# The second block's mixers, reordered: attention units beside the dense tiles, the inverse for two chunk pairs in turn, the state chain beside a two-pass output product, one scale for two norms

## The chip, the cores and the metric
One core of one Trainium2 chip runs the whole program. The metric is the device time of one execution in microseconds (us). Names in the rows: PE is TensorE's matmuls, PEld its weight loads, DVE is VectorE, ACT ScalarE, POOL GpSimd, SP SyncE (it issues the weight loads from memory).

## The reference
Two transformer blocks on 256 tokens (272 with 16 meta tokens in the first) of 1024 features, all in fp32. The change touches only the second block and the norms between the two:

```python
x = first_block(...)                       # ends in rms_norm(h, final_norm)
u = rms_norm(h, norm1_g)                   # the next norm follows at once
p_rwkv, p_nsa = split(u @ w_in)            # 1024 -> 3072 (+ gates)
y = concat([rwkv7_time_mix(p_rwkv), nsa_attention(p_nsa)])
h = h + y @ w_out
h = h + swiglu(rms_norm(h, norm2_g), w_gate, w_up, w_down)
return rms_norm(h, norm_f_g)
```

`rwkv7_time_mix`: 8 heads of 64; per token t the state is `S = S * w_t + (S @ a_t) b_t + v_t k_t`, the output `y_t = S r_t`, then a norm by head, a bonus term and a gate. `nsa_attention`: 8 query and 2 key/value heads; a compressed branch (14 or 15 blocks of 32 tokens), a selected branch and a window branch. With 256 tokens and 4 selection blocks the last two both attend causally to everything; each has a gate per token and head.

## The kernel before
**Layout.** Features lie on the 128 partitions, tokens along the free axis. Every dense product is taken in three fp32r products (`part_products`, L588 to L590: high weight x high activation, high x low, low x high). ScalarE rounds a weight tile of 128x1024 to its high part (`split_hi`, L1247), VectorE subtracts to get the low part (`split_lo`, L1637); four slots hold split tiles, so the splits run four tiles ahead of TensorE. SP fills a ring of two 1 MB blocks (two tiles each), a block being issued when both tiles of the block two before it are split. The small products of the mixers are plain fp32.

**Order.** Five instruction streams are written out by hand and meet by semaphores; each engine runs its stream in order. Around the change they are:

- *Norms.* After the first feed-forward, VectorE adds the down product to `res` (L1875); ScalarE squares each tile twice, plain (L1429) and times the gain norm3 (L1430); TensorE sums both over the partitions (L866, L867). ScalarE takes root and inverse of the first, VectorE multiplies them into the second sum (L1886), ScalarE takes its root, VectorE joins the two scales (L1889). Then VectorE scales tile by tile (L1892), ScalarE rounds, VectorE takes the rest (L1645), and TensorE starts tile 0 of the second projection. VectorE then writes the normed `res` (eight products, L1898) before the first token shift.
- *Second projection, 25 tiles.* Their order is lora and gate inputs, RWKV keys, r and values, then the attention's. TensorE's stream lays RWKV work between tiles: lora products (L900 to L908), head sums (`sums_by_head`, L922), turned tokens and, at tiles 13 to 15, the masked products of each chunk of 64 tokens (L932, L935), then from tile 16 the inverse of a triangular 64x64 matrix per head and chunk in five levels: `join_products(level)`, a copy by ScalarE, `inverse_terms(level)`, an addition by VectorE (L1933, L1936), each for all 4 chunks at once. These are `by_head` products (L886): 32 calls of 64x64 for all chunks, heads two at a time. `hidden` (L970) is the compressed branch's first layer, beside tiles 21 to 24. GpSimd does part of the elementwise work (masks, identity, decays, carried states).
- *After the projection.* Eight attention units (2 branches x 4 query heads per group): scores (L1059, L1063), VectorE's fused bias and maximum (`nsa_maxima`, L2015), ScalarE's exps (L1561), VectorE's scaling of the rows (`nsa_scaled`, L2031), six transposes (L1075), ScalarE's copy (L1596), values (`nsa_values`, L1093), and VectorE's copy out (`nsa_kept`, L2039, L2041). Between the units lie the state's steps, chunk by chunk: `carry_sa`, `sa_grows`, `carry_state`, `state_grows`, and the output of a pair of chunks (`outputs`, L1120 to L1127, `output_sums`, L1133) with its norm, and the compressed branch (L1139 to L1164).
- *Output product.* Eight tiles of the full depth of 8 input tiles, the attended ones first (`MIXER_ORDER`), then the squares of the second norm (L855) and the feed-forward (L603, L605), unchanged by the change.

The lines that carry the inverse before:

```python
by_head(2, lambda c, j: nl[:, c * PAIRS + j, :], lambda c, j, hs: xi[hs, c * PAIRS + j, :])   # join_products
dve.tensor_tensor(xi.rearrange(flat3), both(4), xi.rearrange(flat3), ALU.add)                 # grow
```

## Time and profile before
| | us |
|---|---|
| three runs | 869.26, 864.61, 856.50 |
| median | 864.61 |
| profiled execution | 856.46 |
| its span, first to last instruction | 854.3 |

The span and the 2.2 us around it make the execution's time. The page gives busy time per engine, slices of 21.4 us in tenths, the chain of work that ended last, and groups of instructions by line. A busy TensorE is not one at its peak: the granted clock is 1.0 at 2.4 GHz and 0.5 at 1.2 GHz, and a value between is a mixture over the stretch.

### The profile page before, as it was taken

Reading aid. Unit: us, or ns where it says so; the run is one execution under the profiler, and the core shown is the slowest. Engines: PE = TensorE matmul, PEld = TensorE weight load, DVE = VectorE, ACT = ScalarE, POOL = GpSimd, SP = SyncE. Lnnn points to the kernel's source line nnn. Section 1 sums busy time; section 2 is a strip of 40 time slices with the busy share of each in tenths; the row PEclk is TensorE's granted clock in tenths of the full one; section 3 lists DMA queues with packets and bytes.
Section 4 is the critical chain, followed back from the end, with each engine's and each line's share of the span. In section 5 each row is a group of like instructions: output and inputs, shape, how many; then the busy total and the mean of one; then the engine's idle time right before and its main releaser. Section 6 shows DMA issues by size and latency. Waiting matters only on the chain.

```text
span 854.3 us, 16426 instructions
## 1 busy us (share of the span) xinstructions
PE 783.9 (92%) x6614; PEld 691.8 (81%) x6614; DVE 516.4 (60%) x907; ACT 410.4 (48%) x707; POOL 48.8 (6%) x44
## 2 busy tenths in 40 slices
PE   5999799799999999997989999966589999999996
PEld 4997555398888889996879898854479888889996
DVE  4556433256989995446679442444445999997443
ACT  5334224446656664336763262433445766666332
POOL 0000000000000000000116340010000000000000
PEclk9999778799999999998999999967679999999999
DMA  5644200024765555542333124200114555555541
GB/s 208 248 160 149 86 0 1 0 100 140 259 233 186 208 184 190 196 171 75 100 114 133 52 101 153 99 1 1 50 51 148 197 198 196 179 181 185 193 147 49
DMA packets 16738, 113.65 MB, mean 133 GB/s; under 512 B 2000, under 2 KB 2128, under 8 KB 3632
## 3 DMA queue, kind: packets, MB, share of 16 engines
q1 hardware_dynamic: 15984, 109.22, 36.4%
q0 software_dynamic: 704, 3.71, 1.3%
q8 instruction: 38, 0.62, 0.3%
q14 instruction: 12, 0.10, 0.0%
HBM read 111.87 MB, written 1.05 MB: 132 GB/s over the span
## 4 chain that ended last, share of the span: by engine, by line
PE 82%; DVE 10%; ACT 4%; issue 2%; POOL 1%; DMA 1%; SPq 0%; DVEq 0%; ACTq 0%; POOLq 0%
PE ps L603 19%; PE ps L588 11%; PE ps L590 10%; PE ps L589 10%; PE ps L605 10%; PE ps L886 5%; DVE w_lo L1637 2%; PE ps L1075 1%; ACT w_hi L1247 1%; PE ps L1093 1%; PE ps L743 1%; PE ps L741 1%; PE ps L768 1%; PE ps L855 1%; DVE arena L2015 1%
## 5 line engine op out<-in xcount | busy, mean ns | idle before, releaser
L1637 DVE TENSOR_TENSOR w_lo<-ring,w_hi 128x1024 fp32r<-128x1024 f32 x194 | 248.1, 1279 | 138.2 <-ACT w_hi L1247 136.8
L1247 ACT ACTIVATE w_hi<-ring 128x1024 fp32r<-128x1024 f32 x194 | 204.7, 1057 | 148.2 <-PE ps L590 132.1
L603 PE MATMUL ps<-acts,w_hi 128*128 128x512 f32 x704 | 246.7, 394 | 0.0
L605 PE MATMUL ps<-acts,w_lo 128*128 128x256 f32 x704 | 197.4, 280 | 0.0
L588 PE MATMUL ps<-acts,w_hi 128*128 128x256 f32 (+1 forms) x496 | 149.3, 301 | 18.5 <-DVE acts L1645 13.5
L603 PEld LDWEIGHTS ps<-acts,w_hi 128*128 128x128 f32 x704 | 132.1, 188 | 30.0
L589 PE MATMUL ps<-acts,w_hi 128*128 128x256 f32 (+1 forms) x496 | 144.6, 292 | 0.0
L590 PE MATMUL ps<-acts,w_lo 128*128 128x256 f32 (+1 forms) x496 | 144.6, 291 | 0.0
L605 PEld LDWEIGHTS ps<-acts,w_lo 128*128 128x128 f32 x704 | 132.3, 188 | 0.1
L588 PEld LDWEIGHTS ps<-acts,w_hi 128*128 128x128 f32 x496 | 97.5, 197 | 25.5 <-issue 18.1
L588 PE MATMUL ps<-hid_hi,w_hi 128*128 (+1 forms) x352 | 99.6, 283 | 0.0
L589 PE MATMUL ps<-hid_lo,w_hi 128*128 (+1 forms) x352 | 99.6, 283 | 0.0
L590 PE MATMUL ps<-hid_hi,w_lo 128*128 (+1 forms) x352 | 99.6, 283 | 0.0
L589 PEld LDWEIGHTS ps<-acts,w_hi 128*128 128x128 f32 x496 | 97.8, 197 | 0.5 <-issue 0.5
L590 PEld LDWEIGHTS ps<-acts,w_lo 128*128 128x128 f32 x496 | 97.8, 197 | 0.0
L588 PEld LDWEIGHTS ps<-hid_hi,w_hi 128*128 128x128 f32 x352 | 67.6, 192 | 0.1
L590 PEld LDWEIGHTS ps<-hid_hi,w_lo 128*128 128x128 f32 x352 | 67.6, 192 | 0.0
L589 PEld LDWEIGHTS ps<-hid_lo,w_hi 128*128 128x128 f32 x352 | 67.6, 192 | 0.0
L1403 ACT ACTIVATE hid_hi<-f 128x256 f32 (+1 forms) x44 | 18.4, 419 | 30.3 <-DVE f L1846 30.3
L1396 ACT ACTIVATE yT<-ps 128x256 f32<-128x256 f32 x44 | 16.6, 377 | 23.4 <-PE ps L605 23.4
L1391 ACT ACTIVATE yT<-ps 128x256 f32<-128x256 f32 x44 | 16.6, 378 | 19.0 <-PE ps L605 18.7
L1828 DVE TENSOR_TENSOR yT<-ps,yT 128x256 f32<-128x256 f32 x44 | 18.5, 422 | 8.3 <-ACT yT L1391 8.3
(338 smaller groups left out, 947.0 us busy)
## 6 DMA issues: line engine op xcount, KB each, us to landing
ring<-in_weights SPq DMA_DIRECT2D x101, 1024.0 KB, 4.8
res<-in_xT SPq DMA_DIRECT2D x2, 544.0 KB, 4.3
ring<-in_weights SPq DMA_DIRECT2D x2, 512.0 KB, 4.5
cst<-in_consts POOLq DMA_DIRECT2D x1, 1024.0 KB, 5.4
out_features<-yT SPq DMA_DIRECT2D x4, 256.0 KB, 2.1
cst<-in_consts POOLq DMA_DIRECT2D x1, 817.5 KB, 4.5
vec<-in_vecs POOLq DMA_DIRECT2D x1, 677.5 KB, 4.3
cst<-in_consts POOLq DMA_DIRECT2D x1, 656.0 KB, 5.6
```

The source lines that it names most:

```text
L588: pe.matmul(dst, w_hi[:, slot, k, :], hi, start=first, stop=False, skip_group_check=True)
L589: pe.matmul(dst, w_hi[:, slot, k, :], lo, start=False, stop=False, skip_group_check=True)
L590: return pe.matmul(dst, w_lo[:, slot, k, :], hi, start=False, stop=last, skip_group_check=True)
L603: pe.matmul(ps[:, bank, :].rearrange("p (x t) -> p x t", x=2), w_hi[:, slot, k, :], acts[:, :, k, 0:SEQ], start=(k == 0), stop=(k == KT - ...
L605: return pe.matmul(ps[:, bank, 0:SEQ], w_lo[:, slot, k, :], act_hi[:, k, 0:SEQ], start=False, stop=(k == KT - 1), skip_group_check=True)
L886: mm = pe.matmul(ps[hs, bank + n // 8, (n % 8) * HD:(n % 8 + 1) * HD], lhs(c, j)[hs], rhs(c, j, hs), start=True, stop=True)
L1247: act.activation(w_hi[:, t % SLOTS].rearrange("p k c -> p (k c)"), ring[:, b % RING, half].rearrange("p k c -> p (k c)"), ACT.Copy)\
L1391: act.activation(cross[:, m, 0, :], ps[:, 2 * m, SEQ:2 * SEQ], ACT.Copy).then_inc(S("gate_crossed"), 1)
L1396: act.activation(cross[:, m, 1, :], ps[:, 2 * m + 1, SEQ:2 * SEQ], ACT.Copy).then_inc(S("up_crossed"), 1)
L1403: act.activation(dst, sig2[:, m, :], ACT.Copy).then_inc(S("hid_rounded"), 1)
L1637: dve.tensor_tensor(w_lo[:, t % SLOTS].rearrange("p k c -> p (k c)"), ring[:, b % RING, half].rearrange("p k c -> p (k c)"), w_hi[:, t % S ...
L1828: dve.tensor_tensor(gated[:, m, :], ps[:, 2 * m, 0:SEQ], cross[:, m, 0, :], ALU.add)\
```

## The change
- **Norms.** ScalarE scales the squares with a gain that folds both epsilons (`gain_eps`, made by two small activations behind two small VectorE products), one set of sums gives the one scale that the projection needs. The plain squares go to a buffer of their own; five are made ahead of the root and three between the roundings, their sums are taken by TensorE behind the first and within tile 0. `split_hi` of tile 3 now stands behind the root in ScalarE's stream; VectorE's `split_lo` of it stays ahead of its wait for the root. The eight products that write the normed `res` go under tiles 5, 7, 9 and 11.
- **Projection.** The attention's tiles come right after the gates, RWKV's behind them, the compressed branch's last. The eight units run beside tiles 7 to 25: scores before odd tiles, the turn before even ones, values two odd tiles later. The rows are no longer scaled: the probabilities are the stationary operand, the output comes by token, and VectorE scales its 64-column pieces as it adds them up (`nsa_kept`, before even tiles).
- **RWKV behind the projection.** GpSimd's part goes to VectorE and ScalarE (GpSimd keeps its memsets). The chunk products, then the five levels for two pairs of chunks in turn. VectorE's mask and addition become one masked copy out of PSUM (`copy_predicated`, `fill`) into a matrix that starts as identity. ScalarE copies each token set of a pair in 512 columns (`keep_tokens`, in the order of TensorE's list) and each join (`keep_join`), with one `gather_blocks` ahead of tile 24's copy and one behind it. `hidden` and the compressed branch lie between levels; ScalarE's three activations of its hidden layer stand behind the copy of `key_values(0)`.
- **State chain.** The kept state is added by TensorE (identity product) in place of GpSimd; the decay is applied as VectorE copies out (`keep_state`). The attended sums are transposed back (`nsa_features`).
- **Output product in two passes.** The attended half of the depth goes first, into four banks, beside the state chain; the RWKV half follows. The weight blocks are laid out to match; the second norm's squares and roundings follow in pairs of tiles, six of its eight sums ahead of the first gate product.

```diff
-WA0, G0, GL0, K0, R0, V0, KC0, VC0, VS1, VW1, Q0, KS1, KW1 = 0, 1, 2, 3, 7, 11, 15, 16, 17, 18, 19, 23, 24
-MIXED = 15
+WA0, G0, GL0, KS1, VS1, Q0, KW1, VW1, K0, R0, V0, KC0, VC0 = 0, 1, 2, 3, 4, 5, 9, 10, 11, 15, 19, 23, 24
+MIXED = 14
+OUT2_BANKS = (3, 6, 7, 2)
 TILES2 = 25
@@ TensorE: tiles of the second projection
+            def plain_sum(k):
+                pe.wait_ge(S("plain_squares"), k + 1)
+                mm = pe.matmul(ps[:, 2, 0:SEQ], C("ones"), sq_plain[:, k, :], start=(k == 0), stop=(k == KT - 1),
+                               skip_group_check=True)
+                if k == KT - 1:
+                    mm.then_inc(S("plain_sums"), 1)
+            for k in range(5):
+                plain_sum(k)
...
+            def nsa_values(u):
+                br = u // GQA
+                pe.wait_ge(S("nsa_weights"), u + 1)
+                pe.wait_ge(S("values_kept"), br + 1)
+                if u > 0:
+                    pe.wait_ge(S("nsa_out_kept"), u)
+                for t in range(2):
+                    for g in range(KVH):
+                        dst = ps[:, 7, (t * KVH + g) * HD:(t * KVH + g + 1) * HD]
+                        for kt in range(t + 1):
+                            w0 = (t + kt) * P
+                            mm = pe.matmul(dst, pt_nsa[:, g, w0:w0 + P], vt_nsa[:, br, kt, grp(g)],
+                                           start=(kt == 0), stop=(kt == t), skip_group_check=True)
...
+            pe.wait_ge(S("late_tables_landed"), 48)
+            for t in range(TILES2):
+                if t == 3:
+                    decay_and_rate()
+                if t == 4:
+                    gates()
+                if t == 6:
+                    pe.wait_ge(S("lora_sigmoids"), 1)
+                    turn_values(VS1, True)
+                if t == 12:
+                    turn_values(VW1, False)
+                if t == 14:
+                    pe.wait_ge(S("values_kept"), 2)
+                    pe.wait_ge(S("key_squares"), 2)
+                    sums_by_head(scr, 0, "key_sums")
+                if t == 16:
+                    pe.wait_ge(S("key_sums_kept"), 1)
+                    pe.wait_ge(S("key_squares"), 4)
+                    sums_by_head(scr, 1, "key_sums")
+                if t % 2 and 0 <= (t - 7) // 2 < UNITS:
+                    nsa_scores((t - 7) // 2)
+                if t % 2 == 0 and 0 <= (t - 10) // 2 < UNITS:
+                    nsa_turn((t - 10) // 2)
+                if t % 2 and 0 <= (t - 11) // 2 < UNITS:
+                    nsa_values((t - 11) // 2)
+                pe.wait_ge(S("w_split"), T_IN2 + t + 1)
...
+                        if 2 <= k < 5:
+                            plain_sum(k + 3)
@@ TensorE: the inverse, two chunk pairs in turn
+            def joined(m, level):
+                if level == 1:
+                    pe.wait_ge(S("products_masked"), 2 * m + 2)
+                    if m == 0:
+                        pe.wait_ge(S("tokens_kept"), 1)
+                else:
+                    pe.wait_ge(S(f"xi_grown_{m}"), level - 1)
+                by_head((3, 6)[m], lambda c, j: wtb[:, c * PAIRS + j, 0:HD], lambda c, j, hs: xi[hs, c * PAIRS + j, :],
+                        PAIR[m]).then_inc(S(f"joins_{m}"), 1)
...
+            joined(0, 1)
+            bonus(0)
+            grow_xi(0, 1)
+            joined(1, 1)
+            grow_xt(0, 1)
+            bonus(1)
+            grow_xi(1, 1)
+            joined(0, 2)
+            grow_xt(1, 1)
+            hidden(2)
+            hidden(3)
+            grow_xi(0, 2)
+            joined(1, 2)
+            grow_xt(0, 2)
+            pe.wait_ge(S("bonus_kept"), 2)
+            value_tokens(0)
+            grow_xi(1, 2)
+            joined(0, 3)
+            grow_xt(1, 2)
+            value_tokens(1)
+            cmp_folded()
+            grow_xi(0, 3)
+            joined(1, 3)
+            grow_xt(0, 3)
+            key_values(0)
+            cmp_compressed()
+            grow_xi(1, 3)
+            joined(0, 4)
+            grow_xt(1, 3)
+            key_values(1)
+            grow_xi(0, 4)
+            joined(1, 4)
+            grow_xt(0, 4)
+            turn_tokens(2, ar[:, 0], 1)
+            grow_xi(1, 4)
+            joined(0, 5)
+            pe.wait_ge(S("xi_grown_0"), 4)
+            cmp_scores(0)
+            grow_xt(1, 4)
+            turn_tokens(2, bb, 0)
+            joined(1, 5)
+            grow_xt(0, 5)
+            turn_tokens(2, bb, 1)
+            turn_tokens(2, key_raw, 0)
@@ TensorE: state chain, output product
+            def state_ahead(c):
+                if c > 0:
+                    pe.wait_ge(S("state_grown"), c)
+                    by_head(1, lambda c, j: C("eye64"), lambda c, j, hs: states[hs, c - 1, j, :], (c,), (c % 2) * SEQ,
+                            start=True, stop=False)
+                by_head(1, lambda c, j: k_tok[:, c * PAIRS + j, :], lambda c, j, hs: v_tok[hs, c * PAIRS + j, :], (c,),
+                        (c % 2) * SEQ, start=(c == 0), stop=False)
+            def state_after(c):
+                pe.wait_ge(S("sa_kept"), c + 1)
+                by_head(1, lambda c, j: b_tok[:, c * PAIRS + j, :], lambda c, j, hs: sa[hs, c * PAIRS + j, :], (c,),
+                        (c % 2) * SEQ, start=False).then_inc(S("state_terms"), 1)
...
+            def out_part(half, n, x):
+                t = T_OUT2 + 4 * half + n
+                if x == 0:
+                    pe.wait_ge(S("w_split"), t + 1)
+                for kq in range(4):
+                    k = (4, 0)[half] + kq
+                    mm = part_products(ps[:, OUT2_BANKS[n], x * SEQ:(x + 1) * SEQ], t % SLOTS, 4 * x + kq,
+                                       act_hi[:, k, 0:SEQ], act_lo[:, k, 0:SEQ],
+                                       half == 0 and x == 0 and kq == 0, half == 1 and kq == 3)
+                    if half == 1 and n == 3 and x == 1 and kq < 3:
+                        mm.then_inc(S("act_used"), 1)
...
+            pe.wait_ge(S("tokens_kept"), 8)
+            pe.wait_ge(S("xt_grown_0"), LEVELS - 1)
+            pe.wait_ge(S("cmp_vector"), 3)
+            own_sa(0)
+            own_sa(1).then_inc(S("sa_terms"), 1)
+            from_state(1, 2, 3)
+            turn_tokens(2, key_raw, 1)
+            cmp_turn()
+            pe.wait_ge(S("tokens_kept"), 9)
+            state_ahead(0)
+            pe.wait_ge(S("xt_grown_1"), LEVELS - 1)
+            own_sa(2)
+            own_sa(3)
+            from_state(2, 4, 6)
+            state_after(0)
+            pe.wait_ge(S("tokens_kept"), 10)
+            cmp_values(2)
+            pe.wait_ge(S("w1_kept"), 1)
+            sa_of(1)
+            state_ahead(1)
+            state_after(1)
+            nsa_features(2)
+            pe.wait_ge(S("w1_kept"), 2)
+            sa_of(2)
+            state_ahead(2)
+            outputs(0)
+            state_after(2)
+            pe.wait_ge(S("normed"), normed("mixer2", 3))
+            out_part(0, 0, 0)
+            sa_of(3)
+            out_part(0, 0, 1)
+            output_sums(0, 0)
+            out_part(0, 1, 0)
+            pe.wait_ge(S("sa_kept"), 4)
+            pe.wait_ge(S("y_weighted"), 1)
+            outputs(1)
+            out_part(0, 1, 1)
+            out_part(0, 2, 0)
+            output_sums(1, 4)
+            out_part(0, 2, 1)
+            out_part(0, 3, 0)
+            out_part(0, 3, 1)
+            pe.wait_ge(S("normed"), normed("mixer2", KT - 1))
+            for n in range(4):
+                out_part(1, n, 0)
+                out_part(1, n, 1)
@@ ScalarE: norms
+            act.wait_ge(S("gains_squared"), 1)
+            step(act.activation(gain_eps[:], gain_eps[:], ACT.Ln, bias=C("eps")))
+            step(act.activation(gain_eps[:], gain_eps[:], ACT.Exp, scale=0.5))
             for k in range(KT):
                 act.wait_ge(S("down_added"), k + 1)
-                act.activation(sq[:, k, 0:SEQ], res[:, k, META:CTX], ACT.Square)
-                act.activation(sq_gained[:, k, :], res[:, k, META:CTX], ACT.Square, scale=V("norm3", k))\
+                act.activation(sq_gained[:, k, :], res[:, k, META:CTX], ACT.Square, scale=gain_eps[:, k:k + 1])\
...
+            def plain_square(k):
+                act.activation(sq_plain[:, k, :], res[:, k, META:CTX], ACT.Square).then_inc(S("plain_squares"), 1)
+            for k in range(5):
+                plain_square(k)
+            act.wait_ge(S("norm_sums"), nth("norm3"))
+            step(act.activation(nrm[:, 0, 0:SEQ], ps[:, 3, 0:SEQ], ACT.Ln, bias=C("eps_twice"), scale=1.0 / D))
+            act.activation(nrm[:, 0, 0:SEQ], nrm[:, 0, 0:SEQ], ACT.Exp, scale=-0.5).then_inc(S("norm_root"), 1)
             split_hi(T_IN2 + SLOTS - 1)
-            act.wait_ge(S("norm_squares"), nth("norm3") * KT)
-            act.wait_ge(S("norm_sums"), nth("norm3"))
@@ VectorE: norms
+            dve.tensor_tensor(gain34[:], V("norm3", 0, KT), V("norm4", 0, KT), ALU.mult)
+            dve.tensor_tensor(gain_eps[:], V("norm3", 0, KT), V("norm3", 0, KT), ALU.mult)\
+                .then_inc(S("gains_squared"), 1)
             add_down(1)
             split_lo(T_IN2 + SLOTS - 1)
-            step(dve.tensor_tensor(gain34[:], V("norm3", 0, KT), V("norm4", 0, KT), ALU.mult))
             dve.wait_ge(S("norm_root"), nth("norm3"))
-            signal(dve, dve.tensor_tensor(nrm[:, 0, 0:SEQ], ps[:, 3, SEQ:2 * SEQ], nrm[:, 0, 0:SEQ], ALU.mult),
-                   "norm4_mean")
-            dve.wait_ge(S("norm4_root"), 1)
-            step(dve.tensor_tensor(nrm[:, 0, 0:SEQ], nrm[:, 0, 0:SEQ], nrm[:, 1, 0:SEQ], ALU.mult))
@@ VectorE: units kept, masked fills, end of the mixers
-                else:
-                    dve.wait_ge(S("tokens_kept"), 6)
-                dve.tensor_tensor(states[:, c - 1], ps[:, 3, SEQ:2 * SEQ].rearrange("p (j v) -> p j v", j=PAIRS),
-                                  kvd[:, n, :], ALU.add).then_inc(S("state_grown"), 1)
-            def sa_grows(c):
+                for t in range(2):
+                    for g in range(KVH):
+                        src = ps[:, 7, (t * KVH + g) * HD:(t * KVH + g + 1) * HD]
...
+            def fill(x, mask, m, level, bank):
+                n = slice(2 * m * PAIRS, 2 * (m + 1) * PAIRS)
+                mask = C(mask)[:, level * HD:(level + 1) * HD].bitcast(I32).unsqueeze(1)
+                return dve.copy_predicated(x[:, n, :], mask.to_broadcast([P, 2 * PAIRS, HD]),
+                                           ps[:, bank, :].rearrange("p (n v) -> p n v", n=2 * PAIRS))
...
+            keep_sa(0)
+            keep_state(0)
+            split_lo(T_OUT2 + 1)
+            keep_sa(1)
+            dve.wait_ge(S("cmp_products"), 5)
+            for t in range(2):
+                ins = dve.tensor_tensor(nsa_acc[:, t, :], ps[:, (7, 2)[t], :], nsa_acc[:, t, :], ALU.add)
+            ins.then_inc(S("cmp_vector"), 1)
+            keep_state(1)
+            split_lo(T_OUT2 + 2)
+            keep_sa(2)
+            for a in range(2):
+                rest_attended(a)
+            keep_state(2)
+            for a in range(2, GQA):
+                rest_attended(a)
+            keep_sa(3)
+            y_weighted(0)
             split_lo(T_OUT2 + 3)
-            y_scaled(1)
-            for at in range(1, 4):
-                rest("mixer2", MIXER_ORDER[2][at], SEQ, yT, at)
-            mixer_output(2, T_OUT2)
+            y_finished(0)
+            y_weighted(1)
+            split_lo(T_OUT2 + 4)
+            rest_out(0)
+            y_finished(1)
+            split_lo(T_OUT2 + 5)
+            rest_out(1)
+            split_lo(T_OUT2 + 6)
+            split_lo(T_OUT2 + 7)
+            output_to_gates2()
```

## Rows read from the trace of the kernel before

**Rows 1.** The page: busy time of the engines, then TensorE and its clock in slices.
```profile
PE 783.9 (92%) x6614; PEld 691.8 (81%) x6614; DVE 516.4 (60%) x907; ACT 410.4 (48%) x707; POOL 48.8 (6%) x44
...
PE   5999799799999999997989999966589999999996
...
PEclk9999778799999999998999999967679999999999
```

**Rows 2.** Busy time by stretch: start:end, length, busy of each engine, clock, DMA.
```profile
397.90:403.40 5.50, 5.45 (x25) 5.39 (x26) 5.35 (x15) 3.58 (x7) 0.58 (x1) 0.54 0.00 0
403.40:480.00 76.60, 69.65 (x842) 65.63 (x841) 56.05 (x68) 40.49 (x63) 28.03 (x23) 0.98 0.30 99
444.00:462.00 18.00, 17.26 (x312) 16.42 (x311) 17.91 (x17) 7.24 (x9) 10.71 (x4) 1.00 0.34 119
480.00:542.00 62.00, 62.00 (x1248) 56.97 (x1247) 19.59 (x18) 21.73 (x35) 10.19 (x5) 1.00 0.37 129
557.00:630.50 73.50, 45.68 (x480) 35.20 (x480) 33.98 (x126) 27.14 (x73) 5.00 (x5) 0.70 0.06 20
```

**Rows 3.** Timeline of TensorE: start, length, line; idle before and its releaser.
```profile
397.95 0.55 PE L588 MATMUL ps<-acts,w_hi 128*128 128x256 f32 x1 [5.06 <-DVE acts L1645]
```

**Rows 4.** Chain that ended last, 455 to 545: start, length, engine, line, instructions.
```profile
458.25 0.44 PE ps L932 x8
458.68 0.11 PE ps L935 x4
...
486.65 1.91 PE ps L922 x4
...
507.24 0.31 PE ps L588
...
510.27 5.75 PE ps L886 x192
...
516.02 1.00 PE ps L970 x16
...
541.96 2.01 PE ps L886 x64
```

**Rows 5.** The same chain, 550 to 590.
```profile
550.53 0.42 PE ps L1059 x4
550.95 0.43 PE ps L1063 x4
...
555.45 0.88 PE ps L1075 x6
...
556.94 1.89 PE ps L1156 x32
...
585.95 0.83 PE ps L1093 x12
```

**Rows 6.** Timelines of ScalarE and VectorE, the split of weight tile 3.
```profile
390.50 1.04 ACT L1247 ACTIVATE w_hi<-ring 128x1024 fp32r<-128x1024 f32 x1
...
391.58 1.23 DVE L1637 TENSOR_TENSOR w_lo<-ring,w_hi 128x1024 fp32r<-128x1024 f32 x1 [4.45 <-ACT w_hi L1247]
```

**Rows 7.** VectorE by line and shape, 402 to 660: count | busy, mean ns.
```profile
L1637 DVE TENSOR_TENSOR w_lo<-ring,w_hi 128x1024 fp32r<-128x1024 f32 x32 | 50.0, 1562 | 32.6 <-ACT w_hi L1247 32.5
...
L1933 DVE TENSOR_TENSOR f<-ps,f 128x1024 f32<-128x1024 f32 x4 | 4.9, 1218 | 12.7 <-PE ps L886 12.7
...
L1915 DVE TENSOR_TENSOR arena<-ps,cst 128x512 f32<-128x512 f32 x4 | 2.7, 685 | 0.0
...
L1951 DVE TENSOR_TENSOR_SCAN scratch<-arena,f 128x1024 f32<-128x1024 f32 x1 | 2.3, 2289 | 0.0
```

**Rows 8.** ScalarE's exps (L1561) alone: stretch, length, busy (instructions), clock.
```profile
542.00:630.50 88.50, 14.90 (x64) 0.75 0.07 22
```

**Rows 9.** The chain, 653 to 658.
```profile
654.32 3.02 PE ps L855 x14
```

**Rows 10.** The page: issues of weight blocks, KB each, us to landing.
```profile
ring<-in_weights SPq DMA_DIRECT2D x101, 1024.0 KB, 4.8
```

1260 lines of the change are left out of this document (618 added, 642 removed).

## The prediction

> **What bounds the kernel now.** I read the page first: TensorE is busy 783.9 of 854.3 us and no other engine over 60% [rows 1], so the end moves only if TensorE gets less work, idles less, or runs at its higher clock more. The slices say where it falls short: a few early ones, in a part that the change leaves alone, one near the middle, and four in a row from about 555 to 640 us, with TensorE at 5 to 8 tenths and the clock at 6 or 7 [rows 1]. The table by stretch makes that numbers [rows 2]. From 557.0 to 630.5 TensorE is busy 45.7 of 73.5 us at a mean clock of 0.70; from 480 to 542 it is busy all 62.0 at 1.00. From 403.4 to 480, tiles and mixer work in turn, it idles 6.9 us (76.6 less 69.7). Ahead of tile 0 of the second projection it idles 5.06 us on the norms [rows 3]. In the bad stretch each attention unit is a ring PE, DVE, ACT, PE (scores, maxima, exps, scaling, turn, weights, values) with a wait at each hand-over, and little else lies between.
>
> **Is the work itself less?** Hardly. I price TensorE's blocks at full clock. A dense tile is 3.03 us beside fp32 work (507.24 to 510.27), a "set" of head products (32 fp32 calls, 64 instructions) 2.01 us alone and 1.92 in a run (5.75 for three), a `hidden` 1.0, products of a chunk 2.2 (four times 0.44 and the 0.11 behind it), `sums_by_head` twice 1.91 [rows 4]. An attention unit: scores 0.42+0.43, six transposes 0.88, values 0.83 [rows 5].
> The inverse keeps its 14 sets. The other head products are 9.25 sets before and 10 after (the kept state goes in by an identity product). New are 8 transposes of the attended tokens, 8 x 0.147 = 1.2 us. Compressed values are 8 products of 128 columns before, 2 of 512 after: equal columns. `cmp_folded` halves, under 1 us less. So the work is 1 to 2 us more; the gain must come from lost time.
>
> **Norms before tile 0.** Before: sums of 16 calls at 0.43 from 385.7 end at 392.9, then come Ln, Exp, Exp, product, Ln, Exp, product, scale and round, and the first matmul at 397.95 [rows 3]; DVE scaled the first tile 1.6 before, at 396.35. After: one set of 8 sums. ACT squares each in 0.40 (16 squares alternate from 384.85 to 390.5 when the split starts [rows 6]; those with a gain are the slower), so from 385.2 they end at 388.5; two tiny gain steps are added in front (0.3 us, in the 385.2). Then five plain squares (0.31 each) stand in ACT's queue ahead of Ln: 390.1; Ln and Exp: 391.0. But `split_hi` of tile 3 now stands behind that Exp and DVE has `split_lo` of the same tile ahead of its wait for the root, so both, once hidden under the sums, are on the path: 1.04 and 1.2 us [rows 6], 393.3. First matmul 1.6 later, 394.9: 3.0 us earlier, where 5.3 was to be had. Inside tile 0 three plain sums are added; a clock of 0.54 there [rows 2] makes them 0.86 each, of which the DVE pace of 0.73 per step covers little: +1.6. Tile 0 ends at 402.0, 1.4 us earlier. Bounds: 0 (all eaten) and 3.
>
> **Tile 0's end to tile 24's end**, 403.4 to 541.9 before [rows 2, 4], 138.5 us. Its blocks sum to 129.6 (24 tiles 72.7, 19 sets 36.5, products 8.8, the rest 11.6), so 8.9 were lost, which checks the prices. After: 72.7 + lora and gates 3.5 + turns of values 0.9 + key sums 1.9 + eight scores 6.8 + eight turns 7.0 + seven values 5.8 = 98.6. Do the units fit under two tiles (8.5 us)? ACT: 2 x (0.4+1.05) copies and splits, exps 1.9 (14.9 for eight [rows 8]), weights 0.8 (768 columns at the split's pace), extras 0.5 = 6.1. DVE: splits 2.4, shifts 0.9, maxima 1.7, keeping 1.2, extras 1 to 4: mostly under 8.5, at tiles 17 to 21 just over, which the lead of four split tiles absorbs. The tight link is ACT: behind an odd tile it needs 0.4+1.05+1.9+0.8 = 4.15 us to deliver the weights, and TensorE comes for them after 0.88+3.03+0.85 = 4.76. I add 1 us. The eight norm3 products (3.2 us behind tile 0's rounding), which held up the first shift and with it the tanh, move under tiles 5 to 11; that wait of TensorE, under 1 us, is among the 8.9 lost before and goes. GpSimd's work leaves; in the old mixers splits of 1.2 us [rows 6] took 1.56 in the mean [rows 7]. DVE gains slack by that, no time of its own. Tile 24 ends at 402.0+98.6+1 = 501.6. The cover is thin: without it this stage gives back 13 us (rival 2).
>
> **Tile 24 to the end of the output product**, 541.9 to 654.3 before [rows 4, 9]. After: products 8.8, last values 0.8, 24 sets at 1.94 46.5, `hidden` 4.0, bonus 1.9, compressed branch 5.8, transposes 1.2, outputs 88 calls x 0.063 = 5.5, their sums 1.7, output product 192 x 0.119 = 22.8 [rows 4, 5]: 99.0. In the order of the queues I find these waits: copy of tile 24 behind `gather_blocks` (0.7; five copies of a block's strided columns, 2.7 us); `cmp_compressed` behind ACT's key-value copy and three small activations (2.0); a token copy late (0.6); the first output half behind DVE's last two rests, which are queued behind a state (1.3); `nsa_features` (0.4). Sum 5. Four more hand-overs per step of two chains, not seen by me, get 3. The masked fills (`copy_predicated`, 512 columns from PSUM) stand in no row: below 0.6 (half of the 1024 add at 1.22), above 1.15 (half the scan at 2.29) [rows 7]. I take 0.7, the masked product of 512 columns (0.69), the nearest row. Even 1.15 hides: four fills per level, 4.6 us, under some 8 us of TensorE work, each wanted two blocks later; it shows once, at 0.5. The twelve rounds of level work alternate between the pairs, so each copy (0.6) lies beside a block of 1.0 of the other pair. End: 501.6+99.0+5+3 = 608.6.
> The weights stay ahead: a 1 MB block lands 4.8 us after its issue [rows 10]. SP issues output block 2 when DVE has split the second output tile, about 565, and it is needed from 594 on; the first gate block goes out when output tile 5 is split, about 594, for 612. `hidden` blocks 2 and 3 are issued when the first two are used, about 510, for 522. A load late by its whole 4.8 us would cost 4.8 at one of these places; I book none.
>
> **To the gates.** Six sums of squares, 2.6, then gate products at 611.2 against 657.3 before [rows 9], and two late sums inside instead of one, 0.4. Net 45.7 us. The feed-forward behind (197.0 us to the end) is the same and TensorE-bound.
> Sum: span 854.3 - 45.7 = 808.6, with the 2.2 us around it 810.8 against this execution's 856.5. The median of the three runs is 864.6, 8 us over the profiled one; I take half of that along: **815 us**.
>
> **A rule weighed.** `nsa_values` now loads 128-wide stationary probabilities for 64 moving columns. The group with 128-wide stationaries and only 16 moving columns took 1.89 us for 32 instructions, 59 ns each at clock 1.00 [rows 5]; by that the 12 instructions of a unit take 0.7 to 0.8 us. The Trainium skill (TensorE: Matmul & The Clock Gate, section LDWEIGHTS) has a load take its columns over 1.2, 107 ns for 128: 1.3 us a unit, 3.6 more in all. The trace does not agree.
>
> **Rivals.** (1) The state chain waits at every hand-over as the old ring does. Place: from `own_sa` to the first output half, 14.8 us of work. In 557.0 to 630.5, 31 us of work (by the prices) took 73.5, a factor of 2.3; the same here costs 20: 835. For: same engines, same kind of steps. Against: between two steps of the chain now lie blocks that don't need it.
> (2) The units don't fit under two tiles: seven times one exps pass (1.9 us) late: 13, 828. For: 4.15 against 4.76 leaves 0.6 for every hand-over. Against: the lead of four tiles on all else.
> (3) Both, and the pair chains don't overlap either (18 more, as much again as the chain): 866, about no change; or the change does not do what it says.
> (4) Slower: the granted clock. Between tile 24 and the first output half lie 71 us of small fp32 products with no dense tile. If short gaps put all of it at 1.2 GHz, as about three fifths of 557.0 to 630.5 was (0.70 is that mixture of 1.2 and 2.4), it costs 71: 886. From 50 us on it is slower than before. Against: 444 to 462 is nearly all such work, busy 17.3 of 18.0, at 1.00 [rows 2].
>
> **How the numbers follow.** Forecast 0.66, (1) 0.15, (2) 0.10, (3) 0.06, (4) 0.03. The low end, 803, is the sum without most of my allowances of 9 us (1+5+3) and half of the 8; the high end, 840, holds (1), (2) and slow fills. 2% is about what a measurement of this kernel can tell from no change: 847 and 882. Faster 0.91, within 2% 0.06, slower 0.03.
>
> **What would show it.** Profile after: tile 0 about 3 us earlier with `split_hi`, `split_lo` right in front of it; tile 24 ends near 500 with TensorE busy over 95% and clock 1.00 to there; gates begin near 611; TensorE near 96% of the span, the low-clock slices from 555 gone, GpSimd under 9 us. Wrong if units leave waits of over 0.5 us at each `nsa_values`, fills take over 1.3 us, or the clock between 500 and 580 is under 0.9.

## The result, and the profile after

The changed kernel takes 813.4 us in the median of 4 runs (812.0 to 827.5), the kernel before 866.9 in the same session; the ratio is 0.942, with a 95% interval of 0.930 to 0.953. All ratios here compare fast executions alone, since some executions of either kernel (here the one of 827.5 us) fall in a slower state. Forecast were 815 us and, against the 864.6 us then known, 0.943. A second set of runs of the unedited changed kernel, later and beside other kernels, gave 823.5 us and 0.951 [0.943, 0.959]. So the 815 us owe something to luck: the 4 us that the forecast adds to the profiled execution stand against a scatter of 10 us between two sets of the same kernel.

The page of the changed kernel, parts 1 and 2 in front (busy time by engine; 40 slices of 20.3 us, in tenths):

```profile
PE 774.2 (95%) x6618; PEld 685.8 (84%) x6618; DVE 505.6 (62%) x911; ACT 412.6 (51%) x725; POOL 5.6 (1%) x13
...
PE   6999889979999999999899999989999999999996
...
PEclk9999887769999999999999999999999999999999
```

Against [rows 1]: the four slices at 5 to 8 tenths with the clock at 6 or 7 are gone, and GpSimd's work with them. What is left of a low clock lies in slices 5 to 9, in a part that the change doesn't touch.

That part has to be taken out first, since it differs from execution to execution by more than some of the effects below. The stretch from 60 to 200 us, the same code in all of them, in the changed kernel, in its second profile and in an experiment (`e_gpsimd_spread`, below; start:end, length, busy PE, PEld, DVE, ACT, POOL, clock, DMA share, GB/s):

```profile
60.00:200.00 140.00, 127.66 (x666) 89.38 (x665) 58.29 (x104) 53.76 (x96) 0.00 (x0) 0.83 0.16 57
```
```profile
60.00:200.00 140.00, 127.67 (x591) 85.18 (x591) 53.12 (x97) 48.50 (x86) 0.00 (x0) 0.77 0.13 46
```
```profile
60.00:200.00 140.00, 127.68 (x554) 81.42 (x553) 51.09 (x95) 46.79 (x84) 0.00 (x0) 0.73 0.12 42
```

TensorE is busy equally long in all three, yet does 666, 591 and 554 instructions in that time: the granted clock there is 0.83, 0.77 or 0.73. By the first sum of the norm the profiles stand at 385.7 us (before), 390.7 (after), 399.4 (after, again) and up to 403.8 (an experiment). So I compare a stretch inside each profile, **from the norm's first sum to the first gate product of the second feed-forward**, where all of the change lies. What follows it is 197.3 to 197.7 us in all of them. Five marks in it, each from the timeline of TensorE, counted from the norm's first sum:

```
                       before   forecast   after   six edits more (below)
first product, tile 0    12.2       9.2      8.7      6.4
tile 0 ends              17.7      16.3     15.2      11.7
tile 24 ends            156.2     115.9    112.9
sums of squares begin   268.4     222.9    222.1    213.3
first gate product      271.3     225.5    224.5    215.8
```

The stretch is 46.8 us shorter, of which 45.7 net were forecast. Where they came from, by TensorE's busy time:

```profile
403.40:541.90 138.50, 131.55 (x2086) 122.50 (x2084) 75.64 (x86) 62.22 (x96) 38.22 (x27) 0.99 0.33 112
541.90:654.30 112.40, 82.83 (x942) 70.67 (x942) 56.53 (x178) 46.51 (x118) 6.47 (x7) 0.79 0.14 49
```
These two are of before, tile 0's end to tile 24's, and from there to the sums. The same two stretches after:
```profile
405.97:503.60 97.63, 97.63 (x808) 91.73 (x806) 64.95 (x164) 70.59 (x158) 0.52 (x1) 1.00 0.34 120
503.60:613.10 109.50, 102.58 (x2223) 94.23 (x2223) 56.77 (x105) 41.24 (x77) 0.00 (x0) 0.98 0.24 83
```

Before, TensorE idled 7.0 + 29.6 = 36.5 us here; after, 0.0 + 6.9. That is 29.6 us of the 43.8 between tile 0 and the sums. The other 14.2 is busy time (214.4 less 200.2), although by the forecast's sums the work grew a little. It is time that was busy at half clock: each piece of TensorE's busy time, times what its granted clock lacks to 1.00, adds up to 18.1 us in these two stretches before and 1.7 after.

The waits of over 0.3 us that TensorE has left in the stretch (start, length, line; in brackets idle before and releaser):

```profile
399.46 0.36 PE L533 MATMUL ps<-acts,w_hi 128*128 128x256 f32 x1 [2.85 <-DVE acts L1814]
504.67 0.44 PE L979 MATMUL ps<-arena,scratch 64*64 64x128 f32 x4 [0.99 <-ACT arena L1637]
536.46 0.74 PE L841 MATMUL ps<-scratch,yT 64*64 64x64 f32 x18 [1.20 <-issue]
545.07 0.41 PE L1081 MATMUL ps<-cst,vec 128*64 128x16 f32 x8 [2.00 <-DVE cst L2271]
564.88 1.15 PE L841 MATMUL ps<-cst,arena 64*64 64x64 f32 x32 [0.70 <-ACT arena L1707]
576.98 1.10 PE L1120 MATMUL ps<-cst,yT 128*128 128x128 f32 x8 [0.32 <-DVE yT L2357]
583.61 0.39 PE L533 MATMUL ps<-acts,w_hi 128*128 128x256 f32 x1 [1.19 <-DVE acts L2324]
601.35 0.39 PE L533 MATMUL ps<-acts,w_hi 128*128 128x256 f32 x1 [0.46 <-DVE acts L2348]
```

The reader should hold these beside the forecast's list: tile 24's copy (0.7 forecast, 0.99), `cmp_compressed` (2.0, 2.00), a token copy (0.6, 0.70), the first output half (1.3, 1.19), the features (0.4, 0.32). For the 3 us that it allowed for waits not seen there were 1.20 (`issue`, a gap in the middle of a block, for which the profile shows no releaser) and 0.46. The forecast laid its doubt on one link, ScalarE's copy of a unit's weights and then TensorE's values. Here it is at the fourth and at the sixth unit:

```profile
468.64 0.80 ACT L1610 ACTIVATE arena<-ps 128x768 f32<-128x768 f32 x1
...
470.63 1.55 PE L923 MATMUL ps<-arena 128*128 128x64 f32 x12
...
486.93 0.80 ACT L1610 ACTIVATE arena<-ps 128x768 f32<-128x768 f32 x1
...
488.11 1.55 PE L923 MATMUL ps<-arena 128*128 128x64 f32 x12
```

At the fourth the weights are ready at 469.44 and TensorE comes for them 1.19 us later; at the sixth 0.38 us later. Over the seven units beside dense tiles this slack is 0.47, 0.60, 1.20, 1.20, 0.38, 0.38 and 0.38 us. The forecast had 0.6 (4.15 against 4.76), the right size: the cover held with that little.

### The profile page after: what moved, and what is told of

It is laid out like the page before. It is cut to its first block, busy times and chain, and to the rows that moved or that the text cites. A ratio compares the mean times of both kernels' runs of the same rounds, so it can differ in the third digit from the quotient of the medians.

```text
span 812.9 us, 16425 instructions
## 1 busy us (share of the span) xinstructions
PE 774.2 (95%) x6618; PEld 685.8 (84%) x6618; DVE 505.6 (62%) x911; ACT 412.6 (51%) x725; POOL 5.6 (1%) x13
## 4 chain that ended last, share of the span: by engine, by line
PE 90%; DVE 4%; ACT 3%; issue 1%; DMA 1%; SPq 0%; DVEq 0%; ACTq 0%
PE ps L548 20%; PE ps L533 12%; PE ps L535 12%; PE ps L534 12%; PE ps L550 10%; PE ps L841 5%; PE ps L923 1%; PE ps L690 1%; PE ps L688 1%; PE ps L715 1%; PE ps L979 1%; PE ps L802 1%; PE ps L714 1%; DVE w_lo L1806 1%; ACT w_hi L1338 1%
## 5 line engine op out<-in xcount | busy, mean ns | idle before, releaser
L1806 DVE TENSOR_TENSOR w_lo<-ring,w_hi 128x1024 fp32r<-128x1024 f32 x194 | 237.2, 1224 | 123.6 <-ACT w_hi L1338 122.3
L533 PEld LDWEIGHTS ps<-acts,w_hi 128*128 128x128 f32 x496 | 96.4, 194 | 17.9 <-issue 11.4
L533 PE MATMUL ps<-hid_hi,w_hi 128*128 (+1 forms) x352 | 99.6, 283 | 0.0
L535 PE MATMUL ps<-hid_hi,w_lo 128*128 (+1 forms) x352 | 99.6, 283 | 0.0
L534 PE MATMUL ps<-hid_lo,w_hi 128*128 (+1 forms) x352 | 99.6, 283 | 0.0
```

What stands on the lines that cost most here:

```text
L533: pe.matmul(dst, w_hi[:, slot, k, :], hi, start=first, stop=False, skip_group_check=True)
L534: pe.matmul(dst, w_hi[:, slot, k, :], lo, start=False, stop=False, skip_group_check=True)
L535: return pe.matmul(dst, w_lo[:, slot, k, :], hi, start=False, stop=last, skip_group_check=True)
L1806: dve.tensor_tensor(w_lo[:, t % SLOTS].rearrange("p k c -> p (k c)"), ring[:, b % RING, half].rearrange("p k c -> p (k c)"), w_hi[:, t % S ...
```

## The experiments

Each run is an edit of the changed kernel. "The stretch" is the one above: 224.5 us in the changed kernel, 225.1 in its second profile (`after_again`), so a difference under 0.7 says nothing. That second profile missed what was expected of it, 224.5 within 0.3 us: tile 0 took 5.68 us in it and 6.51 in the first, and it has one more piece at half clock (567 to 571 us). The stretch does depend a little on when the clock falls.

**1. The attention units without the dense tiles.** All eight behind tile 24, two in flight; the calls leave the loop over the tiles on ScalarE and VectorE too:

```diff
-                if t % 2 and 0 <= (t - 7) // 2 < UNITS:
-                    nsa_scores((t - 7) // 2)
...
+            nsa_scores(0)
+            for u in range(UNITS):
+                if u + 1 < UNITS:
+                    nsa_scores(u + 1)
+                nsa_turn(u)
+                if u + 1 < UNITS:
+                    nsa_values(u)
```

> The eight attention units stand behind tile 24, two in flight, with no dense tile between them; all else as in the changed kernel. Theory A (the dense tiles cover the hand-overs): a unit has 3.0 us of TensorE work, and ScalarE needs 1.9 + 0.8 and VectorE 1.7 + 1.2 for it, with about four hand-overs in the ring; I expect 1.5 to 2 us of idle TensorE per unit, 14 us, and a granted clock of about 0.7 over the stretch of some 38 us, which adds about 8: 20 us more in all, ratio 1.025. Rival B (two units in flight cover each other, the dense tiles aren't needed): under 5 us more. Rival C (as bad as before the change, 29.6 us idle and the low clock with it): 40 us more.

Measured: 859.5 us, 0.984 [0.974, 0.994] of the kernel before; the stretch is 263.0 us, **38.5 more**. My theory A, 20, was wrong and C, 40, right in size. TensorE idles 27.6 us in the stretch against 9.7, 17.9 more; the other 20.6 are longer busy time. The timeline of TensorE at one unit, the end of one wait to the end of the next:

```profile
518.60 2.82 PE L923 MATMUL ps<-arena 128*128 128x64 f32 x12 [2.42 <-ACT arena L1611]
...
526.90 2.82 PE L923 MATMUL ps<-arena 128*128 128x64 f32 x12 [2.42 <-ACT arena L1611]
```
and the stretch of the units:
```profile
487.00:545.00 58.00, 39.65 (x187) 31.44 (x187) 16.54 (x102) 20.12 (x72) 0.00 (x0) 0.56 0.00 1
```

A unit takes 8.3 us: 2.42 of idle, and 5.9 of work that is 3.0 at full clock. The clock is 0.56, nearly all at 1.2 GHz.

**2. The same with useless work in the waits**, to part the clock from the waits: two (three) products of 512 columns behind each unit's turn. The edit also has TensorE wait for `key_sums_kept` ahead of the first scores.

```diff
                 nsa_turn(u)
+                for _ in range(2):
+                    pe.matmul(ps[:, 2, :], C("head_ones"), scr[:, 0:2, :].rearrange("p a b -> p (a b)"),
+                              start=True, stop=True)
```

> e_serial_units with two products of no use (head sums of 512 columns into an unused bank, 1.7 us at full clock) in front of the values of each of the eight units, where TensorE waited 2.42 us at 1.2 GHz. In e_serial_units the stretch from the norm's first sum to the first gate product was 263.0 us, 38.5 more than in the changed kernel, with units every 8.3 us. Theory A (a good half of the 38.5 is the low clock: 3.0 us of work per unit doubled): the added work keeps the clock at 1.00, a unit takes 6.2 us or less, and the stretch falls by 12 us or more although TensorE gets 14 us of work added. Rival B (the waits are all there is): the stretch stays within 2 us, as the fill lies in the waits. Rival C (fill adds to the path): it grows by up to 14.

> The same with three useless products per unit, 2.6 us at full clock. Theory A: if two didn't lift the clock, three do; if two did, three cost nothing or up to 0.5 us per unit more than two. Rival B: within 2 us of e_serial_units. Rival C: up to 21 us longer.

Measured: 846.7 and 845.3 us, 0.983 [0.966, 0.999] and 0.981 [0.964, 0.998] of the kernel before. From the 0.984 without useless work these ratios can't be told, two executions each, so the answer lies in the stretch: 252.1 us with two, 252.9 with three, **10.9 and 10.0 us less than with none**, though TensorE has 14 and 21 us more to do. That is theory A, just short of its 12 us. With two:

```profile
514.09 1.55 PE L923 MATMUL ps<-arena 128*128 128x64 f32 x12 [1.36 <-ACT arena L1615]
...
517.14 1.88 PE L1012 MATMUL ps<-scratch,cst 128*128 128x512 f32 x4
520.38 1.55 PE L923 MATMUL ps<-arena 128*128 128x64 f32 x12 [1.36 <-ACT arena L1615]
```
```profile
482.00:531.00 49.00, 39.45 (x232) 25.22 (x230) 17.41 (x106) 21.79 (x75) 0.00 (x0) 0.97 0.00 1
```

A unit now takes 6.29 us at a clock of 0.97. That is the ring of hand-overs itself: three products instead of two lower the wait from 1.36 to 0.51 and leave the pace at 6.29 (508.68 to 514.97 there). So of the 38.5 us at least 10.9 are the low clock; of the other 27.6 some 26 are the ring (6.29 us per unit against 3.0 of work, eight times 3.3). The 20.6 us of longer busy time without the useless work don't all come back, since at full clock TensorE has more of the ring to wait out.

**3. How thick the cover is.** Three more copies of a unit's weights on ScalarE, each waited for, ahead of the one that counts:

```diff
+                for _ in range(3):
+                    step(act.activation(pt_nsa, ps[:, 3:5, 0:P + SEQ], ACT.Copy))
                 act.activation(pt_nsa, ps[:, 3:5, 0:P + SEQ], ACT.Copy).then_inc(S("nsa_weights"), 1)
```

> The changed kernel with three further copies of a unit's weights on ScalarE in front of the one that counts, each 0.8 us and a hand-over to itself: some 2.5 us later per unit. In the changed kernel the weights are ready 1.19 us before TensorE comes for them (469.44 against 470.63). Theory A (that slack is the cover, and beyond it TensorE waits one for one): 1.3 us of wait at each nsa_values, eight times, 10 us more, and the clock may fall with it. Rival B (the delay moves on through ScalarE's queue, copies and splits of the tiles are late as well, ScalarE is full at 6.9 + 2.5 of 9.6 us): over 15 us more. Rival C (the four split tiles of lead absorb it): under 3 us.

Measured: 838.2 us, 0.973 [0.955, 0.991] of the kernel before; the stretch is 247.9 us, **23 more**. The seven waits in front of values of units are 1.3 to 2.1 us (12.9 together; the third and the fifth stand here), and that behind tile 24 grows from 0.99 to 3.42:

```profile
464.62 1.55 PE L923 MATMUL ps<-arena 128*128 128x64 f32 x12 [1.30 <-ACT arena L1612]
...
486.52 1.55 PE L923 MATMUL ps<-arena 128*128 128x64 f32 x12 [2.13 <-ACT arena L1612]
...
520.36 0.69 PE L979 MATMUL ps<-arena,scratch 64*64 64x128 f32 x4 [3.42 <-ACT arena L1639]
```
```profile
400.00:520.00 120.00, 104.06 (x816) 97.45 (x814) 65.59 (x167) 91.21 (x185) 1.40 (x3) 0.95 0.28 97
```

Rival B's number, over 15, but not in the main its mechanism. Each wait and the slack that its unit had before add to 2.5 us (2.4 at the last): beyond the slack TensorE waits one for one, as theory A had it, and its 10 us were low because it took the slack of 1.19 for all units. No wait came up at the dense tiles, though ScalarE is busy 91 of 120 us; what it passes on are the 2.4 us behind tile 24. The rest is the clock: counted as above it costs 11.2 us of the stretch, against 3.4 in the changed kernel. 12.9, 2.4 and 7.8 make the 23. Rival 2 of the prediction, 13 us, priced the waits rightly and left out the clock that they bring.

**4. The chunk pairs in turn or one after the other.** The blocks of TensorE's stream (and ScalarE's and VectorE's to match) put in another order; each call has a line of its own in the code:

```diff
-            joined(0, 1)  bonus(0)  grow_xi(0, 1)  joined(1, 1)  grow_xt(0, 1)  bonus(1)  grow_xi(1, 1)
-            joined(0, 2)  grow_xt(1, 1)  hidden(2)  hidden(3)  grow_xi(0, 2)  joined(1, 2)  grow_xt(0, 2)
+            joined(0, 1)  bonus(0)  grow_xi(0, 1)  grow_xt(0, 1)  bonus(1)
+            joined(0, 2)  hidden(2)  hidden(3)  grow_xi(0, 2)  grow_xt(0, 2)
...
```

> The levels of the inverse are done for chunk pair 0 first, then for pair 1, with the other blocks (bonus, tokens, key values, compressed branch) still spread between them. Theory A (alternating covers copies and fills): of ten joins each then exposes its copy with two hand-overs, 0.9 us, and of eight next joins the fill, 0.7, while some ten side blocks cover about half: 8 us more, 1.010. Rival of the prediction: 18 us more, 1.022. Rival B (side blocks cover it all): under 2 us more.

Measured: 0.949 [0.942, 0.956] of the kernel before; the stretch is 228.8 us, **4.3 more**, half of what I expected and a quarter of the 18 in rival 3. The waits don't even grow: 0.99, 0.56, 1.89, 0.70, 0.70, 0.33, 1.19 and 0.46 are 6.8 us, as much as in the changed kernel. What grows is the time at half clock; here the stretch with most of it:

```profile
540.00:550.00 10.00, 9.21 (x178) 9.03 (x179) 3.44 (x9) 2.62 (x7) 0.00 (x0) 0.66 0.02 5
```

From 540 to 580 the granted clock makes that 10.2 us at 1.2 GHz (0.66, 1.00, 0.94 and 0.89 in stretches of 10 us), where the changed kernel has 3.4 (0.83 from 554 to 564, else 1.00): 6.8 us more at half speed are 3.4 us of the 4.3; another 0.7 lies ahead of tile 24's end, where the edit changes nothing. The low clock sets in right behind the longest gap, the 1.89 us of `issue` that ends at 540.8; in the changed kernel it sets in at 557, 12 us behind the longest one. The side blocks between the levels do the covering, whichever pair they stand in.

**5. The output product beside or behind the state chain.**

```diff
             state_after(2)
-            pe.wait_ge(S("normed"), normed("mixer2", 3))
-            out_part(0, 0, 0)
             sa_of(3)
-            out_part(0, 0, 1)
             output_sums(0, 0)
-            out_part(0, 1, 0)
             pe.wait_ge(S("sa_kept"), 4)
             pe.wait_ge(S("y_weighted"), 1)
             outputs(1)
+            pe.wait_ge(S("normed"), normed("mixer2", 3))
+            out_part(0, 0, 0)
+            out_part(0, 0, 1)
...
```

> The first three parts of the output product stand behind the last chunk's outputs, not between the steps of the state chain; the second pass is untouched. Theory A: sa of chunk 3 waits for the state copy (0.7 us), the last outputs for the copy of sa and the gate product (1.4), and the wait of 1.2 at the first part goes: 1 to 3 us more. Rival 1 of the prediction (each hand-over of the chain costs as the old ring did): over 5 us more even for these two. Rival B: no change within 0.5 us.

Measured: 0.948 [0.942, 0.955]; the stretch is 225.4 us, 0.9 more than the changed kernel's first profile and 0.2 more than its second: about nothing. Waits of 0.53, 0.16 and 1.69 come, those of 1.19 and 0.46 go, 0.7 in balance. Rival 1 (20 us) put the ring's price on this chain; here the hand-overs with nothing in them cost 0.2 and 0.5, and the one to the squares' sum 1.7. The edit bares only the last step of the chain; the steps of chunks 0 to 2 keep the blocks between them, so what those blocks cover wasn't tested.

**6. GpSimd's work put back.** 60 subtractions of 512 columns on GpSimd from the end of tile 0 on; and one at each of 23 tiles.

```diff
+            for t in range(1, 24):
+                pool.wait_ge(S("proj2_ready"), t + 1)
+                step(pool.tensor_tensor(gate_b[:, 0:2, :], gate_b[:, 0:2, :], gate_b[:, 2:4, :], ALU.subtract))
```

> The changed kernel with 60 GpSimd subtractions of 512 columns put beside the dense tiles (from tile 0's end on, some 80 us at 1.3 us each, about twice what GpSimd did there before the change). Theory A (as predicted: without GpSimd VectorE gains slack but no time of its own): split_lo rises from 1.22 toward 1.56 us, VectorE then has 7 to 8 of the 9.6 us per unit, TensorE waits under 1 us in all: no change in the stretch from the norm to the gates. Rival B (VectorE slowed by GpSimd is late with the maxima or the splits): 5 us or more longer.

> The changed kernel with one GpSimd subtraction of 512 columns at each of 23 dense tiles (1.73 us each in e_gpsimd_beside: 40 us in all, near the 38.2 us that GpSimd worked in this stage before the change). e_gpsimd_beside, with 60 of them on end, made the stretch from the norm's first sum to the first gate product 237.0 us, 12 more than the changed kernel's 224.5 to 225.2; there VectorE's instructions with both inputs in SBUF slowed (split_lo 1.22 to 1.60 us, the norm3 products 0.48 to 1.50), those that read PSUM did not. Theory A (the cost is VectorE's lost slack, so it begins only where VectorE is full, 65 of 98.5 us here): this dose costs under 1.5 us. Theory B (in proportion to GpSimd's time, 12 us for some 105): 4.5 us. Theory C (even one late link per unit costs its length): 8 us or more.

Measured: 0.962 [0.954, 0.971] and 0.958 [0.950, 0.965] of the kernel before. With 60 on end (104.1 us of GpSimd) the stretch is 237.0 us, **12.2 more** than the mean of the two profiles without, and my theory for that dose fell. Against the changed kernel's first profile 8.3 us are more idle time and 4.3 the clock. With one per tile (32.0 us) it is 226.3, 1.2 to 1.9 more: for four fifths of the dose that the change took away (38.2 us), "slack, no time of its own" holds but for some 1.5 us. VectorE with the 60, by line; its mean ns stands behind the comma:

```profile
L1811 DVE TENSOR_TENSOR w_lo<-ring,w_hi 128x1024 fp32r<-128x1024 f32 x19 | 30.4, 1598 | 6.1 <-ACT w_hi L1343 6.1
L2168 DVE SCALAR_TENSOR_TENSOR res<-res,vec,nrm 128x256 f32<-128x256 f32 x8 | 11.7, 1496 | 0.0
L2118 DVE CUSTOM_DVE_ANT_0 arena<-ps,cst 128x128 f32<-128x128 f32 (+1 forms) x24 | 7.1, 351 | 0.0
...
L2129 DVE TENSOR_TENSOR cst<-cst 128x4 f32<-128x4 f32 x5 | 5.2, 1044 | 0.2
L2150 DVE SCALAR_TENSOR_TENSOR arena<-ps,cst,arena 128x256 f32<-128x256 f32 x10 | 4.8, 481 | 4.3 <-ACT arena L1637 4.2
```
The first three of these in the changed kernel:
```profile
L1806 DVE TENSOR_TENSOR w_lo<-ring,w_hi 128x1024 fp32r<-128x1024 f32 x21 | 25.7, 1225 | 18.9 <-ACT w_hi L1338 18.8
L2113 DVE CUSTOM_DVE_ANT_0 arena<-ps,cst 128x128 f32<-128x128 f32 (+1 forms) x32 | 9.5, 351 | 0.0
...
L2163 DVE SCALAR_TENSOR_TENSOR res<-res,vec,nrm 128x256 f32<-128x256 f32 x8 | 3.5, 478 | 0.0
```

Instructions that take both inputs from SBUF slow down (1225 to 1598 ns in the mean, 478 to 1496, and a four-column product from 165 to 1044); those with one input from PSUM don't move (351, 481). One with a single input, from SBUF, slows down too, a copy of 16 columns from 165 ns to 1257, while a reciprocal of four columns stays at 170. A small one pays about a microsecond, as much as a large one at most: the splits go from 1.2 us to anything between 1.21 and 2.31. For what they wait the profile doesn't show. The Trainium skill (GPSIMD Engine Reference, section Specifications) says that GpSimd shares its SBUF interfaces with VectorE and contends with VectorE instructions that have two SBUF inputs or run in a 2-port perf mode; on the first half the trace agrees, and whether the copy is a case of the second it doesn't show.

**7. What a product with 128 stationary columns costs.** The shapes of `nsa_values` varied by unit in one kernel:

```diff
+                rows = {2: 64, 4: 64}.get(u, P)
+                cols = {3: 16, 5: 16, 1: P}.get(u, HD)
...
+                                pe.matmul(ps[0:rows, 7, c0:c0 + cols], pt_nsa[:, g, w0:w0 + rows],
+                                          vt_nsa[:, br, kt, v0:v0 + cols], **kw)
```

> The changed kernel with the shapes of nsa_values changed by unit; each keeps its 12 instructions (unit 6: 24). Units 0 and 7 as they are (128 rows by 128 columns stationary, 64 moving: 123 ns each in the changed kernel). Unit 1: 128 moving. Units 2 and 4: 64 stationary columns. Units 3 and 5: 16 moving. Unit 6: each stationary in two halves of 64 rows, the results to two banks. It leaves out half of the output rows of units 2 and 4 and three quarters of the columns of 3 and 5. Theory A (the load of 128 stationary columns sets 123 ns, and the 59 ns of the compressed scores, which have 64 rows, is two loads side by side in two halves of the array): 1.48 us for units 0, 7, 3 and 5, about half (0.75) for 2 and 4, 1.4 to 1.6 for unit 1, and 24 instructions of unit 6 in about 1.5, 61 ns each. Rival B (the moving side sets it): 3 and 5 fall to 0.4 to 0.7, unit 1 rises toward 3, and 2 and 4 stay at 1.48. Rival C (a fixed price of accumulating two products in one place): all stay.

Measured, units 0, 1, 2, 3 and 6 in the timeline of TensorE (each row's length has the modelled drain of its last product in it; the first start to the next tile's first start is the better measure):

```profile
451.16 1.55 PE L933 MATMUL ps<-arena 128*128 128x64 f32 x12
452.52 0.36 PE L533 MATMUL ps<-acts,w_hi 128*128 128x256 f32 x1
460.11 1.61 PE L933 MATMUL ps<-arena 128*128 128x128 f32 x12
...
469.67 0.91 PE L933 MATMUL ps<-arena 128*64 128x64 f32 x12
470.51 0.39 PE L533 MATMUL ps<-acts,w_hi 128*128 128x256 f32 x1
478.73 1.51 PE L933 MATMUL ps<-arena 128*128 128x16 f32 x12
...
480.09 0.36 PE L533 MATMUL ps<-acts,w_hi 128*128 128x256 f32 x1
503.57 1.56 PE L929 MATMUL ps<-arena 64*128 64x64 f32 x24
...
505.06 0.39 PE L533 MATMUL ps<-acts,w_hi 128*128 128x256 f32 x1
```

64, 128 and 16 moving columns: 1.36, 1.37 (the next tile at 461.48) and 1.36 us. Half the stationary columns: 0.84. Theory A: the stationary side alone sets it, 113 ns an instruction for 128 columns and 70 for 64, a little over half. And 24 instructions of half the rows take 1.49, 62 ns each: the 59 ns of [rows 5], whose group has 64 rows too, was two loads side by side, a pace that a 128-row operand doesn't get. The Trainium skill (TensorE: Matmul & The Clock Gate, section LDWEIGHTS) has a load take its columns over 1.2, 107 ns for 128, whatever its rows. For 128 columns the trace agrees within 6 ns, and the prediction, which set the rule aside, read its row wrongly; for 64 columns the rule gives 53 ns and the trace 70.

**8. A version that beats both.** The waits listed above, taken one by one: the third tile's split ahead of the norm's Ln (VectorE makes the first five plain squares); tile 24 copied before the first gather, the last values ahead of the products; the GELU activations ahead of the key-value copy and `cmp_compressed` one block later; a growth product between two token turns; the last rests ahead of the third state.

```diff
-            for k in range(5):
-                plain_square(k)
+            split_hi(T_IN2 + SLOTS - 1)
             act.wait_ge(S("norm_sums"), nth("norm3"))
...
-            keep_tokens(4, 2, kav, 0)
             act.wait_ge(S("cmp_vector"), 1)
...
+            keep_tokens(4, 2, kav, 0)
...
-            for a in range(2):
-                rest_attended(a)
-            keep_state(2)
-            for a in range(2, GQA):
+            for a in range(GQA):
                 rest_attended(a)
+            keep_state(2)
```

> Five edits of order in the changed kernel, each aimed at one wait of TensorE that its profile shows: the split of tile 3 goes ahead of the norm's Ln on ScalarE and ahead of its wait on VectorE, which also makes the first five plain squares (first matmul of tile 0 about 2.2 us earlier); tile 24 is copied before the first gather of blocks, and the last values stand ahead of the products (1.0); the three GELU activations stand ahead of the copy of the key values, and cmp_compressed one block later (2.0); a growth product between two token turns (0.7); the last two rests ahead of the third state (1.2). Theory A (TensorE is the bound here, so each wait is worth its length): 7.1 us less, 0.991 of the changed kernel. Rival B (what follows each wait waits on ScalarE or VectorE itself, so TensorE merely idles a block later): under 3 us less. Each shows in the trace: gone, or turned up behind the next block.

> The five edits of v1_five_waits, and the turn of the compressed weights one block later (behind the first state products), where v1_five_waits showed TensorE waiting 0.98 us for it. From the first sum of the norm to the first gate product the changed kernel took 224.5 us and v1_five_waits 216.5. Theory A (each wait is worth its length): 215.5 here, and 9 us less than the changed kernel in the same call, ratio 0.989. Rival: the wait turns up behind the next block, 216.5.

> The changed kernel itself, unedited, beside v2_six_waits on the same chip: its ratio to the kernel before should come out at 0.94 again, and the stretch from the first sum of the norm to the first gate product at 224.5 us within 0.3, if that stretch doesn't depend on the clock windows of the part ahead of it.

Measured: the stretch is 216.5 us with five edits, 8.0 less (7.1 expected), and 215.8 with six (215.5 expected). With five the kernel takes 813.0 us in the median, 0.933 [0.927, 0.940] of the kernel before. Side by side in one session the version with six takes 811.8 us, 0.939 [0.931, 0.948], and the changed kernel 823.5, 0.951 [0.943, 0.959]: 1.2% less, with intervals that overlap, so the gain rests on the stretch, 8.7 us against the first profile and 9.4 against the second. The waits of over 0.3 us that are left with six:

```profile
394.75 0.36 PE L533 MATMUL ps<-acts,w_hi 128*128 128x256 f32 x1 [0.52 <-DVE acts L1811]
529.11 0.74 PE L841 MATMUL ps<-scratch,yT 64*64 64x64 f32 x18 [1.16 <-issue]
559.95 0.44 PE L1105 MATMUL ps<-cst,arena 128*128 128x128 f32 x2 [0.51 <-DVE arena L2307]
567.11 1.10 PE L1120 MATMUL ps<-cst,yT 128*128 128x128 f32 x8 [0.32 <-DVE yT L2357]
590.22 0.39 PE L533 MATMUL ps<-acts,w_hi 128*128 128x256 f32 x1 [0.46 <-DVE acts L2348]
```

Theory A held in size, and not only by the waits. With five edits the five waits shrank by 7.2 us, but 0.98 turned up at the turn of the compressed weights and 0.3 at `issue`, so TensorE idles 6.0 us less (9.7 to 3.8). Of the other 2 us 1.7 is the clock, which, counted as above, costs 1.7 us of the stretch instead of 3.4. The difference lies in tile 0: behind a wait of 2.85 us 0.74 was granted there and the tile took 6.51 us, behind one of 0.52 us 1.00 was granted and it took 5.32. The sixth edit shows the other side of it: it was made for the wait of 0.98, and it took 0.5 of that away, not all. In the changed kernel TensorE came for those weights just as they were done; an edit that only brings it there sooner makes it wait.

## Why the prediction was right, point by point

**The whole.** 225.5 us forecast for the stretch, 224.5 measured; 810.8 for the profiled execution against 814.7, which is 5.0 more by the norm's first sum, in the part that the change leaves alone, and 1.0 less behind it. That the median of 813.4 lies so near 815 is in part luck: the 4 us booked for the scatter of executions happen to meet those 5.0.

**Norms before tile 0.** Right in mechanism and nearly in size: the first product 8.7 us behind the first sum, 9.2 forecast, with `split_hi` and `split_lo` of tile 3 on the path. Experiment 8 moved them: 2.3 us at the first product, 2.2 expected. Tile 0 ends 2.4 us earlier, 1.4 forecast and 3 its bound. Of the 1.6 us booked for three more sums 1.1 came (6.51 us for the tile against 5.42), and in the second profile 0.3 (5.68): VectorE's last part of tile 0 is done at 404.27, TensorE's products last to 405.97, and how long depends on the clock granted between.

**Tile 0's end to tile 24's end.** 97.6 us, 99.6 forecast. Errors in it cancelled, which is luck. The values of a unit took 1.36 us, not 0.83 (experiment 7), 3.7 more over seven. The 24 tiles took 70.8 us, not 72.7. The six transposes of a turn took 0.57 from first start to the tile's (500.06 to 500.63), not 0.88, 2.5 less over eight; [rows 5] has an old turn behind a wait of 1.71 us, 0.81 by the same measure, and why it is quicker in front of a tile wasn't tested. And the 1 us for lost time wasn't needed.

**Tile 24 to the sums.** 109.5 us, 107.0 forecast. The waits were 6.9 (8 forecast), the fills 0.73 us (0.7 forecast; bounds 0.6 to 1.15):

```profile
L2217 DVE COPY_PREDICATED scratch<-cst,ps 128x512 f32<-128x512 int32 x10 | 7.3, 735 | 8.2 <-PE ps L841 8.1
```

The work came to 102.6 against 99.0: 0.5 of it is the last unit's values, 1.7 is 3.4 us at half clock between 556 and 564 us (0.79 there), and the rest I can't name.

**The rule weighed.** The step that failed: "The trace does not agree." The row had a stationary operand of 64 rows, and `nsa_values` has 128. Rows with the right shape stood in the same profile, in the timeline of TensorE before, ahead of the first unit:

```profile
544.39 1.87 PE L1047 MATMUL ps<-cst,arena 128*128 128x32 f32 x16
546.19 0.49 PE L1059 MATMUL ps<-arena 64*128 64x128 f32 x4
```

16 instructions with 128 rows, 128 stationary and 32 moving columns, 1.80 us from start to start, 113 ns each. The rule's 1.3 us a unit was right.

**The rivals.** (1), 20 us for the state chain, didn't set in; the two hand-overs that experiment 5 bared cost 0.7 us in balance, and the rest of the chain wasn't bared. (2) had the right mechanism and didn't set in, though the slack was as thin as it said, 0.38 to 1.20 us against 0.6; its 13 us were the price of the waits alone, and experiment 3 shows 23 with the clock. (3)'s 18 us for the pairs was four times too much (experiment 4). (4) was right about what the clock can do, wrong about when: experiment 1 has 58 us at 0.56, but behind gaps of 2.4 us in every 8.3; the 80 us of small products from tile 24's end to the first output part, with gaps of at most 2.0 here and there, ran at 0.98.

**GpSimd.** "Slack, no time of its own" is right within 1.5 us for the dose removed and wrong as a rule: 2.7 times as much, on end, costs 12.

**What the parts are worth,** by experiments that undo one each: units beside dense tiles 38.5, the pairs' turns 4.3, the two-pass output 0.2 to 0.9, the norms 3.5 to the first product (from the profile, not undone). They add to 46.5 to 47.2, beside 46.8 measured; with the 1.2 to 1.9 us for GpSimd's work they would be 47.7 to 49.1. That they add so well is partly luck, since each contains some clock, and of the norms' 3.5 only 2.4 are left at tile 0's end.

Not settled: what the `issue` gap of 1.20 us at 536 us is. The changed kernel and all its edits have it at about that block, from 0.95 to 1.89 us; the kernel before has none over 0.6 between the norms and the gates.

## What to carry to other kernels

A chain that goes round three engines (here 6.3 us a turn for 3.0 us of TensorE work) is paid twice on its own, once in waits and once in the clock they bring; put beside work that TensorE does anyway, it costs its work alone, as long as its slowest link stays ahead. Here 0.38 us was enough; measure that margin at every turn of the chain, since one turn in the middle showed three times as much. Beyond the margin each turn waited one for one, and the clock came on top, 7.8 us for 15.3 of waits. Before a row is used as a price, compare the rows of the stationary operand as well as its columns: two 64-row halves run side by side, and a 128-row operand takes the whole load. When runs differ by a per cent in a part that the change leaves alone, compare a stretch between two marks inside the profile: the six-edit version's 9.4 us against the second profile of the changed kernel were plain there.

## What the runs showed of the hardware that was not expected

- GpSimd work beside VectorE delays VectorE instructions with two SBUF inputs, by about 1 us each even when small (165 ns to 1044 for four columns), and one small copy within SBUF (165 to 1257 ns); those that read PSUM keep their times.
- The time of products set by their stationary side doubles with the clock: 12 instructions with 128 columns take 1.36 us at full clock and 2.76 (518.60 to 521.36) at half.
- Useless products in TensorE's waits made the stretch of a kernel 10.9 us shorter.
- A wait of 2.85 us ahead of tile 0 was followed by a granted clock of 0.74 in it, one of 0.52 us by 1.00.
